# Modulation products in a fused two-block kernel: from TensorE to VectorE

## What is computed

```python
m = jnp.split((jax.nn.silu(c) @ w_ada[l] + b_ada[l])[:, None, :], N_MOD, axis=-1)
mc = jnp.split(jax.nn.silu(c_ctx) @ w_ada[l] + b_ada[l], N_MOD, axis=-1)
x = _residual(x, _swiglu(_modnorm(x, g[0], m[0], m[1]), ffn1_w1[l], ffn1_w3[l], ffn1_w2[l]),
              g[1], m[2], HALF_STEP)
h_ctx = _residual(h_ctx, _swiglu(_modnorm(h_ctx, g[0], mc[0], mc[1]), ...), g[1], mc[2], HALF_STEP)
...
# first block, feed-forward
u = jnp.square(jax.nn.relu(rms_norm(x, norm2_w) @ w_up))
return x + u @ w_down
```

## Time and profile before

| | |
|---|---|
| median of 3 runs | 3298.45 us (3293.58 to 3306.25) |
| the profiled execution's own time | 3298.1 us |
| its span in the trace | 3296.0 us |
| mean granted TensorE clock | 0.944 |
| busy: TensorE matmul / VectorE / ScalarE / GpSimd | 90% / 42% / 33% / 1% |
| `w_ada` chunks loaded | 72 of 512 KB, 4.8 us from issue to landing (median) |

### The profile page before, as it was taken

One profiled execution on the slowest core, in us unless ns is written; L12 is line 12 of the kernel. 1 busy time (PEld: TensorE's weight loads), 2 busy tenths in 40 slices (PEclk: granted clock), 3 DMA queues, 4 the chain that ended last, 5 costly groups with the idle time before them and its releaser, 6 DMA issues.

```text
span 3296.0 us, 44230 instructions
## 1 busy us (share of the span) xinstructions
PE 2972.9 (90%) x15161; PEld 2511.1 (76%) x15161; DVE 1391.3 (42%) x2309; ACT 1081.7 (33%) x1597; POOL 35.4 (1%) x27
## 2 busy tenths in 40 slices
PE   6999989899998999968999999499978899599997
PEld 5778777689877778848999999378756577387785
DVE  4335444556644333354323323744444334533334
ACT  3223455332223222234213112422443344442322
POOL 0000000000000000000000000000000000000000
PEclk9999999899999999989999999799989899799997
DMA  3224211344444343421121221011100023133332
GB/s 102 64 76 128 58 51 53 86 123 115 138 133 130 102 115 109 133 70 45 57 64 58 61 60 57 19 39 37 38 19 16 21 67 99 45 90 89 89 90 63
DMA packets 479232, 247.90 MB, mean 75 GB/s; under 512 B 15289, under 2 KB 477578, under 8 KB 479034
## 3 DMA queue, kind: packets, MB, share of 16 engines
q1 hardware_dynamic: 479162, 247.01, 26.3%
HBM read 244.88 MB, written 2.10 MB: 75 GB/s over the span
## 4 chain that ended last, share of the span: by engine, by line
PE 69%; issue 19%; DVE 6%; ACT 4%; DVEq 1%; ACTq 1%; DMA 0%; POOL 0%; POOLq 0%; SPq 0%
PE unit_acc L659 61%; PE aux L862 2%; PE aux L1060 2%; PE aux L1084 1%; PE aux L644 1%; ACT w_hi L1169 1%; DVE w_lo L1655 1%; PE aux L973 1%; PE aux L671 1%; DVE ssq L1673 1%; DVE x L2054 1%; DVE mla_stat L2255 1%; ACT h_hi L1206 1%; PE aux L955 1%; DVEq L2052 0%
## 5 line engine op out<-in xcount | busy, mean ns | idle before, releaser
L659 PE MATMUL unit_acc<-h_hi,w_hi 128*128 128x512 f32 (+2 forms) x2816 | 888.5, 361 | 65.3 <-DVE h_lo L1693 40.3
L659 PE MATMUL unit_acc<-h_lo,w_hi 128*128 128x512 f32 (+2 forms) x2816 | 865.6, 353 | 0.0
L659 PE MATMUL unit_acc<-h_hi,w_lo 128*128 128x512 f32 (+2 forms) x2816 | 864.4, 353 | 0.0
L1655 DVE TENSOR_TENSOR w_lo<-raw,w_hi 128x1024 fp32r<-128x1024 f32 (+3 forms) x405 | 484.8, 1197 | 601.2 <-ACT w_hi L1169 600.2
L1169 ACT ACTIVATE w_hi<-raw 128x1024 fp32r<-128x1024 f32 (+3 forms) x405 | 419.5, 1036 | 905.2 <-PE unit_acc L659 831.9
L659 PEld LDWEIGHTS unit_acc<-h_hi,w_hi 128*128 128x128 f32 x2816 | 504.9, 191 | 156.1 <-issue 52.2
L659 PEld LDWEIGHTS unit_acc<-h_hi,w_lo 128*128 128x128 f32 x2816 | 507.2, 191 | 56.6
L659 PEld LDWEIGHTS unit_acc<-h_lo,w_hi 128*128 128x128 f32 x2816 | 508.5, 191 | 50.3
L659 PE MATMUL unit_acc<-branch_hi,w_hi 128*128 128x512 f32 x448 | 181.8, 406 | 8.0 <-DVE branch_lo L1980 8.0
L659 PE MATMUL unit_acc<-u_hi,w_hi 128*128 128x384 f32 (+1 forms) x528 | 165.4, 368 | 23.0 <-DVE u_lo L2071 23.0
L659 PE MATMUL unit_acc<-branch_lo,w_hi 128*128 128x512 f32 x448 | 180.9, 404 | 0.0
(11 more groups left out here) (285 smaller groups left out, 3095.4 us busy)
## 6 DMA issues: line engine op xcount, KB each, us to landing
raw<-in_w_in_dram SPq DMA_DIRECT2D x132, 512.0 KB, 3.9
raw<-in_ffn_w_dram SPq DMA_DIRECT2D x120, 512.0 KB, 3.8
ada_raw<-in_w_ada_dram SPq DMA_DIRECT2D x72, 512.0 KB, 4.8
raw<-in_w_up_dram SPq DMA_DIRECT2D x32, 512.0 KB, 4.8
raw<-in_w_down_dram SPq DMA_DIRECT2D x32, 512.0 KB, 3.7
raw<-in_w_branch_dram SPq DMA_DIRECT2D x24, 512.0 KB, 3.9
raw<-in_w_out_dram SPq DMA_DIRECT2D x16, 512.0 KB, 3.7
raw<-in_ffn_w_dram SPq DMA_DIRECT2D x16, 384.0 KB, 3.2
```

Source lines behind the costliest of these rows:

```text
L659: last = pe.matmul(G[s][0:n, 512 * j:512 * j + m], w[s][:, k, 0:n], x[:, k, a:a + m], start=(k == 0 and i == 0), stop=(k == kc - 1 and i = ...
L1655: dve.tensor_tensor(wl[s][:, 0:kc, :], raw[s][:, 0:kc, :], wh[s][:, 0:kc, :].bitcast(F32), ALU.subtract).then_inc(lo_split, 1)
```

## The change

All 72 chunks are now worked on VectorE; `ada_unit` is gone. Where both vectors are wanted, `ada_products(j, 2)` runs two sums side by side, in two `ada_sum` tiles (16 operations instead of 8), and `ada_step(j, 2)` makes two products with ones. The order of chunks is now 0 to 71:
- retention: chunks 0 to 7, both vectors, two per head: a sum after the split of unit u+3, ahead of the score products, and one after the split of unit u+5; the two loads per head stand behind weight loads;
- merges and convolution: chunks 8 to 39, both vectors, one per chunk of the stage as before; in the convolution the split of unit u+2 now stands ahead of the sum;
- FF parts 1 to 3: 8 chunks each (40 to 63), `c` alone: 4 in the up phase (in VectorE's iterations n = 0, 2, 4, 6) and 4 in the down phase (n = 0, 2, 4, 6, behind the split, with TensorE's product after unit n+1);
- last FF part: chunks 64 to 71, `c` alone, one in each of the 8 up iterations, TensorE's product for each one unit later, the last after the first down unit;
- the output projection has none.

The FF loops over pairs of units are written out, so that one pass of the loop holds a whole part. The additions and products that make the gains (`ada_gains`) move into the last down phase's first iteration; the context copies stand where they stood.

```diff
 
 
 ADA_BOTH = 5 * KC
-ADA_STEPS = 4 * KC
-ADA_STEP = (0, KC, 3 * KC)
...
         araw = [at(f"ada_raw{s}", AD + s * 4096, [KC, P]) for s in range(2)]
-        asum = at("ada_sum", AD + 2 * 4096, [P])
...
                 for k in range(2, 6):
                     load(Count(U_RET + k, (h, 6)), ret_cols(h, k), KC, P)
+                    if k in (3, 5):
+                        load_ada(Count(k // 4, (h, 2)))
...
             for n in range(KC):
                 load(Count(U_OUT + n), cols("w_out", n * P), KC, P)
-                load_ada(Count(ADA_STEPS + n), Count(n))
...
-            with sp.Fori(0, FF1 // D) as part:
-                with sp.Fori(0, 4) as i:
-                    for e in range(2):
-                        load(Count(U_FF + e, (part, 16), (i, 2)), cols("w_up", part * D + (i * 256 + e * P)), KC, P)
-                        a = Count(KC + e, (part, 8), (i, 2))
-                        load_ada(a + ADA_STEPS, a)
-                with sp.Fori(0, 4) as i:
-                    for e in range(2):
-                        load(Count(U_FF + 8 + e, (part, 16), (i, 2)),
-                             I["w_down"][0, bass.ds(part * D, D), bass.ds(i * 256 + e * P, P)], KC, P)
+            def load_up(part, n):
+                load(count(U_FF + n, (part, 16)), cols("w_up", part * D + n * P), KC, P)
+
+            def load_down(part, n):
+                load(count(U_FF + 8 + n, (part, 16)), I["w_down"][0, bass.ds(part * D, D), n * P:n * P + P], KC, P)
+
+            with sp.Fori(0, FF1 // D - 1) as part:
+                for n in range(KC):
+                    load_up(part, n)
+                    if n % 2:
+                        load_ada(Count(ADA_BOTH + n // 2, (part, 8)))
+                for n in range(KC):
+                    load_down(part, n)
+                    if n % 2:
+                        load_ada(Count(ADA_BOTH + 4 + n // 2, (part, 8)))
+            for n in range(KC):
+                load_up(FF1 // D - 1, n)
+                load_ada(Count(ADA_ALL - KC + n))
+            for n in range(KC):
+                load_down(FF1 // D - 1, n)
...
+            def ada_step(j, both):
+
+                pe.wait_ge(ada_used, val(j + 3))
+                pe.wait_ge(ada_out, val(j + 1))
+                alone(pe, pe_passed)
+                for e in range(both):
+                    last = pe.matmul(A[1][:, 512 + e:513 + e], asum[e][:, :], ones[:, 0:1], start=True, stop=True)
+                last.then_inc(ada_mm, 1)
...
                 unit(u + 3, HH, HL, G1)
+                ada_step(Count(0, (h, 2)), 2)
...
                 unit(u + 5, HH, HL, GM)
+                ada_step(Count(1, (h, 2)), 2)
...
-            def ada_unit(a):
-
-                terms = [(r, 8 * st) for r, st in a.terms]
-                pe.wait_ge(ada_landed[a.slot], val(Count(16 * ((a.base + ADA_STEPS) // 2) + 16, *terms)))
...
-                    last = pe.matmul(dst, araw[a.slot][:, k, :], silu_c[:, k, :], start=(k == 0), stop=(k == KC - 1))
-                last.then_inc(ada_used, 1)
 
...
                 unit(Count(U_OUT + n), MH, ML, GS, ready=(m_lo, 0))
-                ada_unit(Count(n))
             sum_squares(ssq, GS)
 
...
-            def ff_up(part):
-                with pe.Fori(0, 4) as i:
-                    for e in range(2):
-                        unit(count(U_FF + e, (part, 16), (i, 2)), HH, HL, GM, ready=(ap_lo, KC))
-                        ada_unit(count(KC + e, (part, 8), (i, 2)))
...
+            def ff_up(part, final):
+                for n in range(KC):
+                    unit(count(U_FF + n, (part, 16)), HH, HL, GM, ready=(ap_lo, KC))
+                    if final:
+                        if n:
+                            ada_step(Count(ADA_ALL - KC + n - 1), 1)
+                    elif n in (2, 4, 6):
+                        ada_step(Count(ADA_BOTH + n // 2 - 1, (part, 8)), 1)
+
+            def ff_down(part, final):
+                for n in range(KC):
+                    pe.wait_ge(ff_lo, val(count(8, (part, 8))))
+                    unit(count(U_FF + 8 + n, (part, 16)), BH, BL, GS)
+                    if n == 0:
+                        ada_step(Count(ADA_ALL - 1) if final else Count(ADA_BOTH + 3, (part, 8)), 1)
+                    if not final and n % 2:
+                        ada_step(Count(ADA_BOTH + 4 + n // 2, (part, 8)), 1)
...
+            def ada_products(j, both):
+
+                dve.drain()
+                dve.wait_ge(ada_landed[j.slot], val(Count(16 * (j.base // 2) + 16, *((r, 8 * st) for r, st in j.terms))))
+                alone(dve, dve_passed)
+                for k in range(KC):
+                    w = araw[j.slot][:, k, :]
+                    if k:
+                        dve.drain()
+                    for e in range(both):
+                        g = silu_c[:, k, e:e + 1]
+                        if k == 0:
+                            dve.tensor_scalar(asum[e][:, :], w, g, None, ALU.mult)
+                        else:
+                            last = dve.scalar_tensor_tensor(out=asum[e][:, :], in0=w, scalar=g, in1=asum[e][:, :],
+                                                            op0=ALU.mult, op1=ALU.add)
+                last.then_inc(ada_used, 1)
+
+            def ada_copy(j, both):
+
+                dve.wait_ge(ada_mm, val(j + 1))
+                alone(dve, dve_passed)
+                dve.tensor_copy(ada[:, bass.ds(j.value(), 1), 0:both], A[1][:, 512:512 + both].unsqueeze(1)).then_inc(
+                    ada_out, 1)
...
                 split(u + 2)
                 split(u + 3)
+                ada_products(Count(0, (h, 2)), 2)
...
                 split(u + 5)
+                ada_copy(Count(0, (h, 2)), 2)
+                ada_products(Count(1, (h, 2)), 2)
...
                 split(u + 7)
+                ada_copy(Count(1, (h, 2)), 2)
...
-                    ada_products(j)
                     split(u + 2)
+                    ada_products(j, 2)
                     split(u + 3)
...
-            def ff_up(part):
-                with dve.Fori(0, 4) as i:
+            def ff_up(part, final):
+                for n in range(KC):
+                    u = count(U_FF + n, (part, 16))
+                    dve.drain()
+                    dve.wait_ge(ff_r, val(count(1 + n, (part, 8))))
+                    dve.scalar_tensor_tensor(out=sqb[1][:, 0:SEQ], in0=acc(G[u.slot], GM), scalar=0.0,
+                                             in1=sqb[0][:, 0:SEQ], op0=ALU.max,
+                                             op1=ALU.mult).then_inc(evicted[u.slot], 1)
+                    split(u + 2)
+                    dve.drain()
+                    dve.wait_ge(ff_hi, val(count(1 + n, (part, 8))))
+                    dve.tensor_tensor(BL[:, n, :], sqb[1][:, 0:SEQ], BH[:, n, :].bitcast(F32),
+                                      ALU.subtract).then_inc(ff_lo, 1)
+                    if final:
+                        j = Count(ADA_ALL - KC + n)
+                        if n:
+                            ada_copy(j + -1, 1)
+                        ada_products(j, 1)
+                    elif n % 2 == 0:
+                        if n:
+                            ada_copy(Count(ADA_BOTH + n // 2 - 1, (part, 8)), 1)
+                        ada_products(Count(ADA_BOTH + n // 2, (part, 8)), 1)
+
...
+            def ff_down(part, final):
+                for n in range(KC):
+                    u = count(U_FF + 8 + n, (part, 16))
+                    done(u)
+                    x = X[:, n, META:T1]
+                    dve.tensor_tensor(x, acc(G[u.slot], GS), x, ALU.add).then_inc(evicted[u.slot], 1)
+                    split(u + 2)
+                    if final:
+                        add_in_turn(ssq[:, 0:SEQ], sqb, SEQ, 0, n)
+                    if n == 0:
+                        ada_copy(Count(ADA_ALL - 1) if final else Count(ADA_BOTH + 3, (part, 8)), 1)
+                        if final:
+                            ada_gains()
+                    if not final and n % 2 == 0:
+                        ada_products(Count(ADA_BOTH + 4 + n // 2, (part, 8)), 1)
+                    elif not final:
+                        ada_copy(Count(ADA_BOTH + 4 + n // 2, (part, 8)), 1)
+
+            last_part = FF1 // D - 1
+            with dve.Fori(0, last_part) as part:
+                ff_up(part, False)
                 ff_down(part, False)
-            ff_up(FF1 // D - 1)
-
-            dve.wait_ge(ada_used, 2 + ADA_STEPS + ADA_BOTH)
+            ff_up(last_part, True)
             for c in range(KC):
                 dve.wait_ge(ctx_done, c + 1)
                 dve.tensor_copy(X2[:, c, 0:CTX], A[c % 2][:, 0:CTX]).then_inc(ctx_out, 1)
```

More of the change, by code:

```diff
@@ L324, in build @@
         araw = [at(f"ada_raw{s}", AD + s * 4096, [KC, P]) for s in range(2)]
-        asum = at("ada_sum", AD + 2 * 4096, [P])
+        asum = [at(f"ada_sum{s}", AD + 2 * 4096 + s * 512, [P]) for s in range(2)]
         ACT2 = KC * T2 * 4
@@ L513, in load, with load_ada @@
```

(20 more changed lines are left out.)

102 lines of the change are left out of this document (32 added, 70 removed).

## The result

The changed kernel took 3312.03 us (median of 20 runs, 3301.27 to 3326.03), the kernel before 3301.57 us (20 runs, 3292.48 to 3306.25). The ratio is 1.0035, interval 1.0023 to 1.0047: 8 to 16 us slower, clear of noise and inside the 0.5% that the prediction called "the same". The forecast was 3317 us, +19. The 24 us between the two traces are more than twice the 10.5 between the medians, so not all of them belong to the change.

The account below looks back on a forecast made before the run. TensorE was taken to bound merges, output projection and FF up phases, except at an up phase's end, where it waits for VectorE's `branch_lo`. Terms -47.5 + 7.5 + 9.3 + 6.0 + 2.1 + 37.2 + 4.5 = +19.1 gave 3317.2 us, range 3297 to 3334.

Parts of the forecast that it names:

- F: Last up phase: sum, weight load, splits and next sum form a ring, 13.1 us a turn against 7.39; +37.2 us.
- A: TensorE: 40 chunk multiplications of 1.68 us removed, 28 of them on the path; -47.5 us.
- B: TensorE: second products in retention, merges and convolution, and products in FF parts 1 to 3, added; +7.5 us.
- E: End of up phases 1 to 3: VectorE reaches unit 7 late, `branch_lo` 0.7 later, three times; +2.1 us.
- C: Retention and merges: double sums of 5.3 us delay what stands behind them; +9.3 us.
- D: Down phases of FF parts 1 to 3: TensorE waits 0.5 us for a sum, twelve times; +6.0 us.
- G: TensorE's granted clock falls after stops in retention and at the start of the last down phase; +4.5 us.
- Rival 1: Last up phase: the ring isn't closed, because the loads are early enough; 3276 us, chance 0.12.
- Rival 2: F holds, but the short waits don't: C, D and G fall to about 2 together; 3299 us, chance 0.20.
- rival 3: F holds, double sum near 6.5, every retention stop lowers the clock, second products at 0.21; 3329 us, chance 0.18.

Follow-up runs that it names:

- e1: Changed kernel with modulation load n issued behind weight load n+2 in the last FF part (SyncE's order only); 3279.7 us, ratio 0.9936 to the kernel before.
- e6: Changed kernel with six of the eight operations of each sum in the last FF part left out; 3294.93 us, ratio 0.9983 to the kernel before.
- e4: Changed kernel with GpSimd's two memsets at the start of block 2 waiting for VectorE's first copy into ssq; 3306.67 us, ratio 1.0023.
- e7: Kernel before the change with GpSimd's two memsets waiting for VectorE's first copy into ssq; 3296.46 us, ratio 0.9984.
- e3: Changed kernel with three of four products in the down phases of FF parts 1 to 3 taken one unit later; 3302.54 us, ratio 1.0010.

## Why the prediction was right

The forecast was the mechanism F with small stops elsewhere, and that mechanism is what the traces and e1 and e6 show. The size was met less well: +19.1 was forecast, and +10.5 is the difference of the medians. The forecast put 0.48 on "slower" and 0.40 on "the same", and the same it was, by its own line of 0.5%. Term by term, in us, from the traces:

| term | forecast | measured |
|---|---|---|
| A, output projection | -11.8 | -11.9 |
| A, B, E: up phases 1 to 3 | -32.6 | -34.0 |
| B: second products, merges and convolution | +4.4 | +6.6 |
| C: retention | +6.8 | +6.5 |
| C: first chunks of merges 0 and 2 | +2.5 | +1.9 |
| D, with its products | +7.8 | +11.4 |
| F: last up phase | +37.2 | +34.2 |
| G: clock | +4.5 | -0.2 |
| sum | +18.8 | +14.5 |

(The forecast column lacks 0.3 of the 19.1: retention's products and rounding.) The measured 14.5 lie inside the 8 to 16 of the interval and beside the 13 of e4 over e7. That the forecast sum is within 5 us of it is in part luck: F and G were put 7.7 too high, B and D 5.8 too low. What else separates the two profiled executions is no part of the change: 5.1 us the copy; 1.0 at the start, where the first weight landed later; some 2 around the differential attention, whose code is the same (the first head ran at a granted clock of 0.89 where the trace of before shows 1.00; among the changed kernel's variants e3 and e6 took the 30.1 us of before for that head, so this too varies from run to run); the last 1 is in block 2, which took 1829 to 1846 us in ten traces.

**F** was right in mechanism and within 3 us in size. A turn is 12.35 instead of 13.1: SyncE issues 0.02 after the sum's end, not 0.23, and the weight takes 5.2 to 5.4, not 5.65. The 0.23 had been read behind a split and did not hold for a sum. Six such turns would have given F about 32; the sixth took 14.5, which the sum did not have, and gave 2 back.

**C** was right where it was doubtful. The double sum was put at 5.3 from one pair of independent operations; it is 5.31, and the stop that follows from it 1.65 a head, forecast 1.7. The Trainium skill (VectorE: DVE Perf Modes, "The DRAIN you can't avoid") says that the next operation waits until the pipe is empty, and, which the prediction left out, that one that is not held starts earlier. The trace agrees with the second: in the double sum a pair takes 0.68 us, in a single sum the dependent operations follow at 0.43, so the second of a pair adds 0.25 and not its whole 0.35.

**D** is the term that was mis-sized. Its wait of 0.5 was about right (0.38 to 0.47 in the rows); that a stop costs its wait alone was wrong. TensorE loses 0.54 between the last matmul and the product, 0.23 for the product, and 0.09 in the first matmuls behind it. A down phase got 3.6 to 3.9 longer by four of them and one product without a wait; e3 shows what that costs, 0.21.

**B** took 0.15 for a second product; it costs 0.21 to 0.23, the upper bound named. The 0.12 for a first one was the length of its row in the chain; by e3 it takes 0.21 of TensorE's time.

**G** was put at 4.5 and came to nothing. The four stops in retention left the clock at 1.00, and the last down phase, which starts after a wait in both traces, took 0.2 us less than before. Longer waits did lower it, in both kernels: in the one before, the clock was 0.50 (1.2 GHz) over the 6 us behind the 2.65 us wait ahead of the third down phase, and in the changed one 0.66 over the 8.6 us behind the 4.76 us wait at the same place. The stall at a taken branch, for which the prediction had left 2 us out, can be seen at most as 0.36 and 0.40 us of "issue" ahead of the first unit of parts 2 and 3, where the long loop branches back; at part 4, behind the loop, it is 0.02. That the branch causes it was not tested.

Rival 1 (the ring isn't closed, 3276) described the kernel of e1, 3279.7, and was rightly seen to turn on one point, SyncE's order. Rival 2 (3299) and rival 3 (3329) fell with the double sum at 5.3; of rival 3 the second products at 0.21 came true, its clock did not.

Left open: what decides whether the copy gets in between the memsets, and why block 2 varies: e4 and e7 have the same code there and the copy at 0.56, and took 1828.6 and 1839.4 us.

## What to carry to other kernels

An engine's queue that serves two streams closes a ring when a load of the one waits for work that itself stands behind a load of the other; the busy shares (VectorE 48%, TensorE 89%) show nothing of it, the order of the DMA issues beside the ends of the work they wait for does. Issuing the modulation loads two weight loads later left the rest of the program as it was and gave 32 us here. Work that is put on an idle engine did best here dealt out one piece per two units, with its result fetched a unit later than it could be: eight sums in one up phase made it 34 us longer than eight multiplications on TensorE had, and each step fetched a unit late, without a wait, costs TensorE 0.2 us.

## What the runs showed of the hardware that was not expected

A matmul stream that is stopped for a wait of 0.38 us loses 0.86, of which 0.23 is the inserted product itself. Two memsets on GpSimd held a VectorE copy of 0.56 us for 3.04 or 8.19 us, at the same starts, a difference of 5 us from one execution to the next: by the medians, a wait that puts them in order was worth 2 us in the kernel before (3298.9 to 3296.5; by the ratio 5, clear of noise) and 5 in the changed one (3312.0 to 3306.7, not clear of noise).
